# A decoder layer with a mixture of experts: the second half of each expert's weight splitting is moved from VectorE to GpSimd

## The chip, the core and the metric

The kernel runs on one core of a Trainium2 chip, as one program. TensorE (PE in the rows; PEld is its weight load), VectorE (DVE), ScalarE (ACT), GpSimd (POOL) and SyncE (SP) run their own instruction streams and wait for one another by semaphores. The metric is device time in microseconds. Three runs of the kernel before gave 1063.22, 1064.2 and 1065.08 us, a median of 1064.2 us.

## The reference, cut to what matters

One layer: a parallel attention and mLSTM mixer, then a mixture of experts over 1024 tokens of 1024 values, with 16 experts of hidden width 512 and two experts for each token, all in float32. The change lies in the experts:

```python
def hier_moe(x, w_rg, b_rg, w_re, b_re, w_gate, w_up, w_down):
    ...                                  # routing: 2 of 16 experts for each token
    y = jnp.zeros(t.shape, jnp.float32)
    for e in range(N_EXPERTS):
        h = jax.nn.silu(t @ w_gate[e]) * (t @ w_up[e])
        y = y + combine[:, e:e + 1] * (h @ w_down[e]).astype(jnp.float32)
```

## The kernel before, in words

The attention, the mLSTM and the routing take the first 590 us or so and are not touched. Then the experts are worked through in order, 0 to 15. The tokens of an expert are gathered into tiles of 128 rows; an expert has at least one tile. With this input there are 24 tiles: experts 1 to 5, 7, 11 and 12 have two, the other eight (0, 6, 8, 9, 10, 13, 14, 15) have one.

Every product of float32 numbers is made of three matmuls on a high part and a low part (`three`): high by high, high by low, low by high. So each weight is split before it is used. An expert's weights are 12 pieces of 128x1024 values: pieces 0 to 7 are gate and up in turn, pieces 8 to 11 are the four row blocks of the down matrix. For each piece of the next expert:

- SP loads it into a slot (`load_piece`), once the low part of the piece that was there is made (`lo_ready`). SP goes through the pieces in order, so a late piece 11 also holds back the load of the next piece 0.
- ACT copies it, rounded, into `whi` (`w_high` in the rows), once PE has done its last matmul with the piece that `whi` held (`split_hi`, the semaphore `act_hi`).
- DVE subtracts the rounded value from the exact one into `wlo` (`w_low`; `split_lo`, L1628, L1632). Both inputs of this instruction are in SBUF: the slot and `whi`.

All this is done in the last tile of an expert, for the expert that follows; where an expert has two tiles, nothing is split in its first. There are 15 such tiles. The order of a tile on DVE is written out in `tile` (L1635): the product of activation and up for hidden columns 0 to 255 (`hidden`, L1606, `q_sb` in the rows), piece 0, the low part of that half (`hidden_lo`, L1619), piece 1, the other half's product and low part, the low parts of the next tile's rows (`rows_lo`, L1613), pieces 2 to 7, the weighting of the tile's result (`weigh`, L1626), pieces 8 to 11. Pieces 8 to 11 are therefore split while PE is already in the next tile.

PE's tile (L1155) is 24 matmuls of 128x512 for gate and up of hidden columns 0 to 255 (bank J0), 12 of the 24 for the other columns (bank J1), the transposes of the first half of the hidden values (`hidden_T`, L1151, `bank_s`), the other 12, the eight transposes of the next tile's rows (`rows_T`), the transposes of the second half (`bank_x`), and 24 for the down product, six for each of pieces 8 to 11. Before each pair of gate and up pieces and before each down piece it waits for the low part.

POOL's tile (L598) picks the row numbers of the tile after the next, waits until PE has transposed the rows that are in the buffer, issues the gather, waits for the weighted result of ACT and DVE, picks this tile's row numbers and issues the scatter that adds the result into the output. Each wait on a register value is followed by a multiply of one element (`tick`, L525).

Of the kernel before, what the change touches and what calls it, by code (L numbers as in the profile page):

```python
# [5 lines left out]
def hymba_layer_program(nc, x, rel_bias, norm_mix_g, w_in, q_norm_g, k_norm_g, attn_sink, conv_w, conv_b,  # L6
# [15 lines left out]
    F32 = mybir.dt.float32  # L22
# [3 lines left out]
    ALU = mybir.AluOpType  # L26
# [25 lines left out]
    FC = FF // P  # L52
# [11 lines left out]
    with ctx:  # L64
        def sb(name, shape, dt=F32):
            return ctx.enter_context(nc.sbuf_tensor(name, shape, dt))
# [4 lines left out]
        def sems(names):  # L71
            return [ctx.enter_context(nc.semaphore(n)) for n in names.split()]
# [14 lines left out]


        PIECES, PW = 3 * FC, 2 * FF
        OUTP = D // P  # L90
        whi, wlo = sb("w_high", [P, PIECES * PW], F32R), sb("w_low", [P, PIECES * PW], F32R)

        mxh, mxl = sb("rows_high", [P, KC, P], F32R), sb("rows_low", [P, KC, P], F32R)

        MX = [(mxh, mxl), tuple(w[:, OUTP * PW:(OUTP + 1) * PW].rearrange("p (k n) -> p k n", k=KC)
                                for w in (whi, wlo))]
# [6 lines left out]
        def sb1(name, shape):  # L103
# [98 lines left out]
        slot = [*pieces_of(wres, 6), slot_b[:, 0:PW], junk, gffn[:, :], xin[:, 0, :], xin[:, 1, :], h2[:, :]]  # L202
# [39 lines left out]
        (hi0, lo0, act_hnh, dve_hnl) = sems("hi_proj lo_proj act_hn_high dve_hn_low")  # L242

        ld_piece = sems(" ".join(f"ld_piece{j}" for j in range(PIECES)))
        (ld_rows, ld_g, st_y, act_hi, lo_ready_w, pe_mx, pe_gup, pe_hT, pe_dnp, act_silu, act_mx, act_hT, act_y,
         dve_mh, dve_mx, dve_hT, dve_y, pool_rowg, dve_wt) = sems(
            "ld_rows ld_gathered st_y act_hi lo_ready_w pe_mx pe_gateup pe_hT pe_down act_silu act_mx act_hT act_y "
            "dve_mh dve_mx dve_hT dve_y pool_rowg dve_wt")

        block = ctx.enter_context(nc.Block())  # L250
# [1 line left out]
        def wait(eng, sem, value):  # L252

            if not (isinstance(value, int) and value <= 0):
                eng.wait_ge(sem, value)
# [59 lines left out]
        def order(i):  # L315

            return (i % 2) * FC + i // 2 if i < 2 * FC else i

        def lo_ready(e, i):


            return (lo_ready_w, e * PIECES + (i + 1))

        def split_free(i):

# [4 lines left out]
        def _(sp):  # L330
# [68 lines left out]
            def body(t, u, main, nxt, ahead):  # L399
                if main and not nxt:  # L400
# [4 lines left out]
                    sp.wait_ge(dve_hn, TILES)  # L405
                    for i in range(OUTP):
                        if i == OUTP - 1:
                            sp.wait_ge(lo0, PIECES + 1)
# [11 lines left out]
            sp.dma_start(xin[:, 0, :], x2[0:P, :]).then_inc(LDX[0], 16)  # L420
            sp.wait_ge(lo0, PIECES + OUTP)
            sp.dma_start(gffn[:, :], norm_ffn_g[0, :].partition_broadcast(P)).then_inc(ld_gf, 16)
# [61 lines left out]
        def _(pool):  # L484
# [35 lines left out]
            def pwait(sem, value):  # L520

                pool.wait_ge(sem, value)
                if not isinstance(value, int):
                    ticks.append(len(ticks))
                    pool.tensor_tensor(tick[:, len(ticks):len(ticks) + 1], mhalf[0:1, 0:1], mhalf[0:1, 0:1], ALU.mult)  # L525
# [40 lines left out]
            def gather():  # L566
                pool.indirect_dma_start(
                    out=xg[:, :], out_offset=None, in_=ffn_in,
                    in_offset=bass.IndirectOffsetOnAxis(ap=row_g[:, 0:1].bitcast(U32), axis=0)).then_inc(ld_g, 16)

            def scatter_add():
                pool.indirect_dma_start(  # L572
                    out=out, out_offset=bass.IndirectOffsetOnAxis(ap=row_s[:, 0:1].bitcast(U32), axis=0),
                    in_=yb[:, :], in_offset=None, compute_op=ALU.add).then_inc(st_y, 16)

            def pick(dst, t):

                at = tabi[0:1, ROWS + t:ROWS + t + 1] if isinstance(t, int) else tabi[0:1, bass.ds(t + ROWS, 1)]
                col = pool.value_load(at, min_val=0, max_val=TCOLS - 1)
                pool.tensor_copy(dst[:, :], rows[:, bass.ds(col, 1), 0:1].rearrange(  # L580
                    "p a c -> p (a c)")).then_inc(pool_rowg, 1)
# [13 lines left out]
            gather()  # L595
            pool.wait_ge(st_h, 16 * TILES)

            def tile(t):  # L598
                pwait(ld_g, 16 * t + 32)
                pick(row_g, t + 2)  # L600
                pwait(pool_rowg, 2 * t + 3)
                pwait(pe_mx, t + 2)
                gather()
                pwait(act_y, t + 1)
                pwait(dve_y, t + 1)
                pick(row_s, t)
                pwait(pool_rowg, 2 * t + 4)
                scatter_add()

            def inner_tiles(e):  # L610
                first = pool.value_load(tabi[0:1, FIRST + e:FIRST + e + 1] if isinstance(e, int) else
                                        tabi[0:1, bass.ds(e + FIRST, 1)], min_val=0, max_val=MAXT - 1)
                last = pool.value_load(tabi[0:1, LAST + e:LAST + e + 1] if isinstance(e, int) else
                                       tabi[0:1, bass.ds(e + LAST, 1)], min_val=0, max_val=MAXT - 1)
                with pool.If(first < last):
                    with pool.Fori(first, last) as t:
                        tile(t)
                return last

            with pool.Fori(0, NE - 1) as e:  # L620
                tile(inner_tiles(e))
            end = inner_tiles(NE - 1)
            tile(end)
            pwait(st_y, 16 * end + 16)
            pwait(ld_g, 16 * end + 48)

# [2 lines left out]
        def _(act):  # L629
# [16 lines left out]
            def out_high(i):  # L646

                act.wait_ge(ld_piece[i], 32)
                act.wait_ge(pe_om, TILES)
                act.activation(whi[:, i * PW:(i + 1) * PW], slot_out[i], ACT.Copy,  # L650
                               scale=gml[:, i - AW // P:i - AW // P + 1] if i >= AW // P else 1.0).then_inc(hi0, 1)
# [21 lines left out]
            def body(t, u, main, nxt, ahead):  # L673
# [37 lines left out]
                if main:  # L711
# [6 lines left out]
                    if not nxt:  # L718
                        for i in range(4, OUTP):
                            out_high(i)  # L720
# [104 lines left out]
            def split_hi(e, i, last):  # L825

                act.wait_ge(ld_piece[i], e * 16 + (48 if i < OUTP else 32))
                if last is not None:
# [370 lines left out]
        def _(dve):  # L1199
# [402 lines left out]
            def hidden(t, half):  # L1602
                cols = slice(half * HF, (half + 1) * HF)
                dve.wait_ge(act_silu, 2 * t + half + 1)
                wait(dve, pe_hT, 2 * t)
                dve.tensor_tensor(mh[:, cols], sg[:, cols], (J0, J1)[half][:, HF:], ALU.mult).then_inc(dve_mh, 1)  # L1606
# [9 lines left out]
            def hidden_lo(t, half):  # L1616
                dve.wait_ge(act_hT, 2 * t + half + 1)
                at = slice(2 * half, 2 * half + 2)
                dve.tensor_tensor(mhl[:, at, :].rearrange("p a b -> p (a b)"), (S0, X0)[half][:, 0:HF],  # L1619
                                  mhh[:, at, :].bitcast(F32).rearrange("p a b -> p (a b)"), ALU.subtract).then_inc(dve_hT, 1)  # L1620
# [14 lines left out]
            def tile(t, split):  # L1635
                wait(dve, act_y, t)
                wait(dve, dve_y, t)
                col = dve.value_load(tabi[0:1, bass.ds(t + ROWS, 1)], min_val=0, max_val=TCOLS - 1)
                dve.tensor_copy(wt_t[:, 0:1], rows[:, bass.ds(col, 1), 1:2].rearrange("p a c -> p (a c)")
                                .bitcast(F32)).then_inc(dve_wt, 1)  # L1640
                hidden(t, 0)
                split(0, 1)
                hidden_lo(t, 0)
                split(1, 2)
                hidden(t, 1)
                hidden_lo(t, 1)
                rows_lo(t + 1)
                split(2, 2 * FC)
                weigh(t)
                split(2 * FC, PIECES)  # L1650

            def inner_tiles(e):
                first = dve.value_load(tabi[0:1, FIRST + e:FIRST + e + 1] if isinstance(e, int) else
                                       tabi[0:1, bass.ds(e + FIRST, 1)], min_val=0, max_val=MAXT - 1)
                last = dve.value_load(tabi[0:1, LAST + e:LAST + e + 1] if isinstance(e, int) else
                                      tabi[0:1, bass.ds(e + LAST, 1)], min_val=0, max_val=MAXT - 1)
                with dve.If(first < last):
                    with dve.Fori(first, last) as t:
                        tile(t, lambda a, b: None)
                return last  # L1660

            for i in range(2 * FC):
                split_lo(0, i)
            rows_lo(0)
            for i in range(2 * FC, PIECES):
                split_lo(0, i)
            dve.wait_ge(ld_rows, 16)
            with dve.Fori(0, NE - 1) as e:
                last = inner_tiles(e)

                def split(a, b):
                    for i in range(a, b):
                        split_lo(e + 1, i)
# [44 lines left out]
```

## Time and profile before

| | |
|---|---|
| median of three runs | 1064.2 us |
| the profiled execution, its own time | 1064.2 us |
| its span | 1062.4 us |
| PE busy | 948.8 us, 89% |
| DVE busy | 618.2 us, 58% |
| ACT busy | 527.4 us, 50% |
| POOL busy | 246.2 us, 23% |

The span is the time from the first to the last instruction of the core in the profiled execution; the 1.8 us between it and the time are the start and the end of the program. The busy shares are means over the whole program, and the stretch that the change touches is the last 450 us of it. Of the DMA traffic, 169.68 MB in all, the most is weights of the experts: 16 experts of 12 pieces of 512 KB. Spans on POOL are rough.

### The profile page before, as it was taken

The numbers are of one execution on the slowest core, as the hardware profiler recorded it, in microseconds if no ns is written. First come the engines' busy times: TensorE is split into PE (matmuls) and PEld (weight loads), VectorE is DVE, ScalarE is ACT, GpSimd is POOL, SyncE is SP. The second block draws the span as 40 slices with busy tenths as digits, with TensorE's granted clock in tenths as the row PEclk, the third lists the DMA queues.
The fourth block names the chain that finished last, engine by engine and source line by source line (L and its number), as shares of the span: only waits on it lengthen the run. The fifth ranks groups of instructions, "written<-read, shape, count | busy, mean of one in ns | idle before, by whom it ended". The sixth has DMA issues, their size and how long they took to land. (4 is left out here: it accounts for less than half of the span.)

```text
span 1062.4 us, 16918 instructions
## 1 busy us (share of the span) xinstructions
PE 948.8 (89%) x5026; PEld 792.8 (75%) x5027; DVE 618.2 (58%) x1245; ACT 527.4 (50%) x945; POOL 246.2 (23%) x362
## 2 busy tenths in 40 slices
PE   4789999999999969699971799999999999999993
PEld 3678889898888857588861577877877777787772
DVE  3646555656665565343367466447639489754891
ACT  3364644627455373122114356545638488664871
POOL 3101001010110100000017133243234345513452
PEclk9999999999999986899985799999999999999998
DMA  8620010101000050533463788678669799966963
GB/s 259 216 54 20 22 40 0 39 0 39 20 20 20 2 190 9 172 126 134 142 220 102 288 285 255 166 231 289 177 202 339 220 319 395 374 174 202 321 245 60
DMA packets 58122, 169.68 MB, mean 160 GB/s; under 512 B 12744, under 2 KB 15088, under 8 KB 58096
## 3 DMA queue, kind: packets, MB, share of 16 engines
q1 hardware_dynamic: 50384, 143.13, 37.5%
q0 software_dynamic: 7712, 26.24, 10.5%
q8 instruction: 13, 0.21, 0.1%
q14 instruction: 13, 0.11, 0.0%
HBM read 142.96 MB, written 26.38 MB: 159 GB/s over the span
## 5 line engine op out<-in xcount | busy, mean ns | idle before, releaser
L886 PE MATMUL bank_j<-w_high,rows_high 128*128 128x512 f32 x640 | 256.6, 401 | 11.7 <-DVE w_low L1327 9.4
L888 PE MATMUL bank_j<-w_high,rows_low 128*128 128x512 f32 x640 | 251.4, 393 | 0.0
L887 PE MATMUL bank_j<-w_low,rows_high 128*128 128x512 f32 x640 | 251.3, 393 | 0.0
L886 PEld LDWEIGHTS bank_j<-w_high,rows_high 128*128 128x128 f32 x640 | 121.2, 189 | 40.9 <-issue 12.3
L525 POOL TENSOR_TENSOR tick<-mhalf 1x1 f32<-1x1 f32 x146 | 83.9, 577 | 279.1 <-ACT lg L823 136.8
L888 PEld LDWEIGHTS bank_j<-w_high,rows_low 128*128 128x128 f32 x640 | 121.2, 189 | 26.1
L887 PEld LDWEIGHTS bank_j<-w_low,rows_high 128*128 128x128 f32 x640 | 121.6, 190 | 23.7
L1632 DVE TENSOR_TENSOR w_low<-w_res,w_high 128x1024 fp32r<-128x1024 f32 x96 | 112.8, 1219 | 13.8 <-ACT w_high L633 13.8
L633 ACT ACTIVATE w_high<-w_res 128x1024 fp32r<-128x1024 f32 x96 | 96.2, 1059 | 8.4 <-PE bank_j L888 8.0
L880 PE MATMUL bank_t<-ident,hn 128*128 128x128 f32 x328 | 45.1, 283 | 33.8 <-DMA hn<-ffn_in,row_g 22.2
L880 PEld LDWEIGHTS bank_t<-ident,hn 128*128 128x128 f32 x328 | 40.0, 146 | 39.0 <-issue 34.8
L982 PE MATMUL bank_j<-hnT,w_res 128*128 128x128 f32 x512 | 63.7, 285 | 1.5 <-DMA w_res<-in_w_in_dram 1.5
L982 PEld LDWEIGHTS bank_j<-hnT,w_res 128*128 128x128 f32 x512 | 61.9, 201 | 2.8 <-DMA w_res<-in_w_in_dram 1.9
L1606 DVE TENSOR_TENSOR q_sb<-cy,bank_j 128x256 f32<-128x256 f32 x48 | 20.1, 419 | 71.1 <-ACT cy L803 71.1
L530 POOL TENSOR_TENSOR rqk<-ssqk,eps_hd 128x10 f32<-128x10 f32 x8 | 5.8, 728 | 224.8 <-DVE ssqk L1423 224.8
L803 ACT ACTIVATE cy<-bank_j 128x256 f32<-128x256 f32 x48 | 18.1, 377 | 72.1 <-PE bank_j L888 72.1
L572 POOL DMA_INDIRECT out_dram<-lg,row_s x24 | 50.6, 2108 | 5.9 <-issue 5.9
L669 ACT ACTIVATE lg<-lg,anm 128x256 f32<-128x256 f32 x64 | 31.7, 497 | 34.1 <-DVE aes L1352 34.1
L633 ACT ACTIVATE w_high<-bias 128x1024 fp32r<-128x1024 f32 x36 | 36.3, 1065 | 7.5 <-DMA bias<-in_w_in_dram 7.5
L886 PE MATMUL bank_s<-w_high,hidden_high 128*128 128x512 f32 x96 | 39.9, 416 | 0.0
L633 ACT ACTIVATE rows_high<-bank_t 128x512 fp32r<-128x512 f32 x58 | 31.4, 599 | 15.2 <-PE bank_t L880 15.2
L1632 DVE TENSOR_TENSOR w_low<-bias,w_high 128x1024 fp32r<-128x1024 f32 x32 | 37.7, 1222 | 0.0
(301 smaller groups left out, 1823.0 us busy)
## 6 DMA issues: line engine op xcount, KB each, us to landing
w_res<-in_w_gate_dram SPq DMA_DIRECT2D x48, 512.0 KB, 4.9
w_res<-in_w_up_dram SPq DMA_DIRECT2D x48, 512.0 KB, 5.4
bias<-in_w_down_dram SPq DMA_DIRECT2D x32, 512.0 KB, 5.6
slot_b<-in_w_gate_dram SPq DMA_DIRECT2D x16, 512.0 KB, 5.7
PT<-in_w_up_dram SPq DMA_DIRECT2D x16, 512.0 KB, 5.9
gmix<-in_w_down_dram SPq DMA_DIRECT2D x16, 512.0 KB, 5.5
h<-in_w_down_dram SPq DMA_DIRECT2D x16, 512.0 KB, 7.2
hn<-in_x_dram SPq DMA_DIRECT2D x8, 512.0 KB, 3.5
```

Of the source, the lines that this page charges most:

```text
L525: pool.tensor_tensor(tick[:, len(ticks):len(ticks) + 1], mhalf[0:1, 0:1], mhalf[0:1, 0:1], ALU.mult)
L572: pool.indirect_dma_start(out=out, out_offset=bass.IndirectOffsetOnAxis(ap=row_s[:, 0:1].bitcast(U32), axis=0), in_=yb[:, :], in_offset=No ...
L633: return act.activation(dst, src, ACT.Copy)
L669: act.activation(pr[:, j, :], lg[:, j, :], ACT.Exp, bias=anm[:, h:h + 1], accum_out=asum[:, h:h + 1])
L803: act.activation(sg[:, half * HF:(half + 1) * HF], (J0, J1)[half][:, 0:HF], ACT.Silu).then_inc(act_silu, 1)
L880: ins = pe.transpose(TB[b][:, i * P:(i + 1) * P], src[:, (4 * b + i) * P:(4 * b + i + 1) * P], ident[:, :])
L886: pe.matmul(out_, ah, bh, start=start, stop=False)
L887: pe.matmul(out_, ah, bl, start=False, stop=False)
L888: return pe.matmul(out_, al, bh, start=False, stop=stop)
L982: ins = pe.matmul(J0[:, c * P:(c + 1) * P], wi[:, k, KVG + c * P:KVG + (c + 1) * P], hnT[:, k, :], start=(k == 0), stop=(k == KC - 1))
L1606: dve.tensor_tensor(mh[:, cols], sg[:, cols], (J0, J1)[half][:, HF:], ALU.mult).then_inc(dve_mh, 1)
L1632: dve.tensor_tensor(wlo[:, at], slot[i], whi[:, at].bitcast(F32), ALU.subtract).then_inc(lo_ready(e, i)[0], 1)
```

## The change

The low parts of pieces 8 to 11 of experts 1 to 15 are made by POOL, and no longer by DVE. POOL makes them behind the scatter of the tile in which DVE made them. Those of expert 0 stay on DVE. The low parts have two semaphores, `lo_a` for pieces 0 to 7 and `lo_b` for pieces 8 to 11, each with a count of its own, since two engines now signal them. The instruction is the same: 128x1024 values, one input in the slot and one in `whi`.

```diff
+        VP = 2 * FC
...
         def lo_ready(e, i):
-            return (lo_ready_w, e * PIECES + (i + 1))
+            return (lo_a, e * VP + (i + 1)) if i < VP else (lo_b, e * (PIECES - VP) + (i - VP + 1))
...
-            def tile(t):
+            def tile(t, split):
                 pwait(ld_g, 16 * t + 32)
                 pick(row_g, t + 2)
                 pwait(pool_rowg, 2 * t + 3)
                 pwait(pe_mx, t + 2)
                 gather()
+                split(VP, 2 * FC)
                 pwait(act_y, t + 1)
                 pwait(dve_y, t + 1)
                 pick(row_s, t)
                 pwait(pool_rowg, 2 * t + 4)
                 scatter_add()
+                split(2 * FC, PIECES)
...
             with pool.Fori(0, NE - 1) as e:
-                tile(inner_tiles(e))
+                last = inner_tiles(e)
+
+                def split(a, b):
+
+                    for i in range(a, b):
+                        pool.wait_ge(act_hi, e * PIECES + (PIECES + i + 1))
+                        at = slice(order(i) * PW, order(i) * PW + PW)
+                        pool.tensor_tensor(wlo[:, at], slot[i], whi[:, at].bitcast(F32),
+                                           ALU.subtract).then_inc(lo_ready(e + 1, i)[0], 1)
+                tile(last, split)
...
-                split(2, 2 * FC)
+                split(2, VP)
                 weigh(t)
-                split(2 * FC, PIECES)
```

`VP` is 8, as `2 * FC` is, so the first `split` on POOL is empty and the second makes pieces 8 to 11. The last lines are those of `tile` on DVE.

POOL's stream at the end of an expert's last tile, before: the tile's result is waited for, its row numbers are picked (`row_s`), the scatter is issued, and the loop over the experts turns (L620, L611).

```order
L525 TENSOR_TENSOR tick<-mhalf 1x1 [waits dve_y]
L579 ISA
L579 TENSOR_LOAD tabi
L579 ISA x2
L580 ISA
L580 COPY row_s<-rows 128x1
L522 REGISTER_ALU
L525 TENSOR_TENSOR tick<-mhalf 1x1 [waits pool_rowg]
L572 DMA out_dram<-lg,row_s 1152x1024
L620 REGISTER_ALU
```

The same place in the changed kernel, from the last tick before the scatter:

```order
L526 TENSOR_TENSOR tick<-mhalf 1x1 [waits pool_rowg]
L573 DMA out_dram<-lg,row_s 1152x1024
L629 ISA
L631 TENSOR_TENSOR w_low<-gmix,w_high 128x1024 [waits act_hi]
L629 REGISTER_ALU
L631 TENSOR_TENSOR w_low<-bias,w_high 128x1024 [waits act_hi]
L629 REGISTER_ALU
L631 TENSOR_TENSOR w_low<-bias,w_high 128x1024 [waits act_hi]
L629 REGISTER_ALU
L631 TENSOR_TENSOR w_low<-h,w_high 128x1024 [waits act_hi]
L623 REGISTER_ALU
```

Four subtractions of 128x1024 stand between the scatter and the turn of the loop, and so ahead of the next tile's gather.

DVE's stream at the same end of a tile, before, from the weighting of the result (`lg`) on:

```order
L1626 TENSOR_SCALAR lg<-bank_o,wt_t 128x512 [waits st_y]
L1630 REGISTER_ALU
L1632 TENSOR_TENSOR w_low<-gmix,w_high 128x1024 [waits act_hi]
L1630 REGISTER_ALU
L1632 TENSOR_TENSOR w_low<-bias,w_high 128x1024 [waits act_hi]
L1630 REGISTER_ALU
L1632 TENSOR_TENSOR w_low<-bias,w_high 128x1024 [waits act_hi]
L1630 REGISTER_ALU
L1632 TENSOR_TENSOR w_low<-h,w_high 128x1024 [waits act_hi]
L1668 REGISTER_ALU
```

And in the changed kernel:

```order
L1644 TENSOR_TENSOR w_low<-PT,w_high 128x1024 [waits act_hi]
L1635 REGISTER_ALU
L1637 REGISTER_ALU [waits dve_wt,pe_down]
L1638 TENSOR_SCALAR lg<-bank_o,wt_t 128x512 [waits st_y]
L1679 REGISTER_ALU
```

The four subtractions behind the weighting are gone; the loop turns right after it, and the next instructions with work are the copy of the weights and the first `hidden` product of the next tile.

## Rows read from the trace of the kernel before

**Rows 1.** busy by stretch: length, PE PEld DVE ACT POOL, clock, DMA, GB/s

```profile
604.00:1050.00 446.00, 426.55 (x1983) 345.89 (x1981) 293.01 (x370) 276.33 (x392) 167.32 (x237) 1.00 0.79 259
857.10:876.40 19.30, 18.20 (x86) 14.67 (x85) 17.20 (x21) 15.99 (x22) 9.55 (x10) 1.00 1.00 352
912.90:950.20 37.30, 36.17 (x170) 29.45 (x169) 21.22 (x30) 20.55 (x31) 12.45 (x20) 1.00 0.76 246
```

**Rows 2.** waits: line, what it waited for: us, times, longest

```profile
PE bank_s L1151 <- DVE q_sb L1606: 15.5, 15, 1.1
```

**Rows 3.** the chain that ended last: start, us, what

```profile
866.50 0.44 PE bank_s L1151 x2
```

**Rows 4.** timeline of PE: start, us, engine, line, what [idle before]

```profile
857.13 0.39 PE L886 MATMUL bank_j<-w_high,rows_high 128*128 128x512 f32 x1
866.50 0.44 PE L1151 MATMUL bank_s<-ident,q_sb 128*128 128x128 f32 x2 [1.05 <-DVE q_sb L1606]
870.61 0.44 PE L1151 MATMUL bank_x<-ident,q_sb 128*128 128x128 f32 x2
870.81 0.49 PE L886 MATMUL bank_s<-w_high,hidden_high 128*128 128x512 f32 x1
876.39 0.39 PE L886 MATMUL bank_j<-w_high,rows_high 128*128 128x512 f32 x1
```

**Rows 5.** timeline of DVE, the same tile

```profile
860.76 0.75 DVE L1626 TENSOR_SCALAR lg<-bank_o,wt_t 128x512 f32<-128x512 f32 x1
861.42 1.22 DVE L1632 TENSOR_TENSOR w_low<-gmix,w_high 128x1024 fp32r<-128x1024 f32 x1
864.83 1.22 DVE L1632 TENSOR_TENSOR w_low<-h,w_high 128x1024 fp32r<-128x1024 f32 x1
866.35 1.22 DVE L1632 TENSOR_TENSOR w_low<-w_res,w_high 128x1024 fp32r<-128x1024 f32 x1
870.13 0.42 DVE L1606 TENSOR_TENSOR q_sb<-cy,bank_j 128x256 f32<-128x256 f32 x1 [1.09 <-ACT cy L803]
871.99 1.29 DVE L1613 TENSOR_TENSOR rows_low<-bank_t,rows_high 128x512 fp32r<-128x512 f32 x2
873.20 4.62 DVE L1632 TENSOR_TENSOR w_low<-w_res,w_high 128x1024 fp32r<-128x1024 f32 x4
```

**Rows 6.** timeline of ACT, the same tile

```profile
863.72 0.36 ACT L803 ACTIVATE cy<-bank_j 128x256 f32<-128x256 f32 x1
864.13 2.01 ACT L633 ACTIVATE w_high<-w_res 128x1024 fp32r<-128x1024 f32 x2
```

**Rows 7.** timeline of POOL while DVE splits

```profile
861.59 1.10 POOL L525 TENSOR_TENSOR tick<-mhalf 1x1 f32<-1x1 f32 x1 [1.83 <-DVE lg L1626]
862.64 1.18 POOL L580 COPY row_s<-rows 128x1 int32 x1
```

**Rows 8.** timeline of DVE, then POOL, where the expert has a second tile

```profile
708.33 0.75 DVE L1626 TENSOR_SCALAR lg<-bank_o,wt_t 128x512 f32<-128x512 f32 x1 [3.40 <-PE bank_o L888]
710.73 1.60 POOL L572 DMA_INDIRECT out_dram<-lg,row_s  x1 [0.39 <-issue]
```

**Rows 9.** POOL by form: count, busy us, mean ns, idle before

```profile
L530 POOL TENSOR_TENSOR hrs<-hss,eps_dv 128x4 f32<-128x4 f32 x8 | 1.6, 203 | 122.5 <-DVE hss L1475 122.5
L530 POOL TENSOR_TENSOR rsh<-ssh,eps_d 128x1 f32<-128x1 f32 x8 | 1.5, 189 | 116.8 <-ACT PT L791 116.8
L497 POOL TENSOR_SCALAR_AFFINE_SELECT selh<-selh 4x512 f32<-4x512 f32 x1 | 0.6, 634 | 0.1
L501 POOL TENSOR_SCALAR_AFFINE_SELECT selp<-selp 4x256 f32<-4x256 f32 x1 | 0.4, 407 | 0.1
```

**Rows 10.** DMA issues: KB each where known, median us to landing

```profile
h<-in_w_down_dram SPq DMA_DIRECT2D x16, 512.0 KB, 7.2
hn<-ffn_in,row_g POOLq DMA_INDIRECT x26, 5.3
```

**Rows 11.** the scatter on POOL: count, min/median/max ns, first and last start

```profile
L572 POOL DMA_INDIRECT out_dram<-lg,row_s x24: 1584/2407/2435, 622.2 to 1049.9; - x24
```

More of the change, by code:

```diff
@@ L244, in hymba_layer_program @@
         ld_piece = sems(" ".join(f"ld_piece{j}" for j in range(PIECES)))
-        (ld_rows, ld_g, st_y, act_hi, lo_ready_w, pe_mx, pe_gup, pe_hT, pe_dnp, act_silu, act_mx, act_hT, act_y,
+        (ld_rows, ld_g, st_y, act_hi, lo_a, lo_b, pe_mx, pe_gup, pe_hT, pe_dnp, act_silu, act_mx, act_hT, act_y,
          dve_mh, dve_mx, dve_hT, dve_y, pool_rowg, dve_wt) = sems(
-            "ld_rows ld_gathered st_y act_hi lo_ready_w pe_mx pe_gateup pe_hT pe_down act_silu act_mx act_hT act_y "
+            "ld_rows ld_gathered st_y act_hi lo_a lo_b pe_mx pe_gateup pe_hT pe_down act_silu act_mx act_hT act_y "
             "dve_mh dve_mx dve_hT dve_y pool_rowg dve_wt")
@@ L616, in inner_tiles @@
                     with pool.Fori(first, last) as t:
-                        tile(t)
+                        tile(t, lambda a, b: None)
                 return last
             with pool.Fori(0, NE - 1) as e:
-                tile(inner_tiles(e))
+                last = inner_tiles(e)
[6 more added lines that the diff above has]
+                tile(last, split)
             end = inner_tiles(NE - 1)
-            tile(end)
+            tile(end, lambda a, b: None)
             pwait(st_y, 16 * end + 16)
@@ L1660, in inner_tiles @@
                 return last
-            for i in range(2 * FC):
+            for i in range(VP):
                 split_lo(0, i)
             rows_lo(0)
-            for i in range(2 * FC, PIECES):
+            for i in range(VP, PIECES):
                 split_lo(0, i)
```

## The prediction

> **What bounds the kernel now.** I read the busy time by stretch first. In the 446 us of the experts PE is busy for 426.55 us at a granted clock of 1.00, the higher of its two levels (2.4 GHz), DVE for 293.01 and POOL for 167.32 [rows 1]. PE sets the time, then, and only what PE waits for counts. The list of waits names one such wait in this stage: the transposes of the first half of the hidden values wait for DVE's product, 15 times, 15.5 us in all [rows 2]. Fifteen is the number of tiles that come right behind a tile in which weights were split. The chain that ended last goes through the same transposes [rows 3].
>
> The timelines of one tile show why. PE starts it at 857.13 and stands still for 1.05 us before 866.50 [rows 4]. DVE had the result weighted at 860.76 to 861.51, then split pieces 8 to 11, the last from 864.83 to about 865.96, and only then could make the product, though ACT's half of it was there at 863.72 + 0.36 = 864.08 [rows 5, 6]. PE wanted the product by 866.50 - 1.05 = 865.45. The tile takes 876.39 - 857.13 = 19.26 us, 1.05 of which is the gap, so 18.2 without it [rows 4].
>
> **What the change removes.** Four subtractions of about 1.14 us (861.42 to the next DVE work at 864.83 is three of them, 3.41 us) leave DVE ahead of the product [rows 5]. The product can then be made as soon as ACT is ready, 864.1 to 864.5, which is 0.9 us ahead of PE. ACT's own work is unchanged and comes no later. The whole gap of 1.05 us closes, in 15 tiles: -15.8 us. Behind it the next limit is PE itself.
>
> **What it adds: when POOL can start.** POOL splits behind the scatter. Where DVE does not split, the scatter is issued at 710.73 and ends at 712.33, which is 3.25 us after DVE ended the weighting (708.33 + 0.75 = 709.08) [rows 8]. In the changed kernel DVE is idle there too, so in the tile above POOL starts piece 8 at 861.51 + 3.25 = 864.76.
>
> **How long one piece takes on POOL.** The trace has no such instruction. From below: one with a single input costs 634 ns for 512 elements and 407 for 256, 0.887 ns an element, so 0.18 + 0.91 = 1.09 us for 1024. From above: the addition of two inputs costs 203 ns for 4 elements and 189 for 1, 4.7 ns an element, so 5.0 us for 1024 [rows 9]. The first slope is taken over 256 elements and the second over three, so I stay near the first: with two inputs read one behind the other it gives 0.18 + 2 x 0.91 = 2.0 us. With 0.3 us for starts, ends and the handing over from piece to piece, I take 2.3 us as the spacing, an estimate. The Trainium skill (GPSIMD Engine Reference, Elementwise side by side) has 4497 ns for a two-input addition of 2048 elements, so an estimate of 2.25 us for 1024; the sum below would be about 1 us lower by it. No row here shows it.
>
> **What lies behind POOL's pieces.** PE needs piece 8 + c at the c-th step of the down product. That product is 24 matmuls in 876.39 - 870.81 = 5.58 us, 0.2325 each [rows 4]. Without the gap it starts at 869.76 and asks for piece 11 after 18 matmuls, at 873.95. POOL has piece 11 at 864.76 + 4 x 2.3 = 873.96. So at 2.3 us a piece it just fits; each 0.1 us more costs 0.4 us in each tile, and at 2.56 us the gain of 1.05 is used up. POOL's gather comes 5 us later than now, lands in 5.3 us [rows 10], and is read a tile of 18 us later: hidden. SP's load of piece 11 waits for POOL and lands 7.2 us later [rows 10]. If POOL ends at 876.2 (below), it lands at 883.4, about 1.5 us late for ACT in a one-tile expert, inside PE's new slack of 0.9 and a little more. I count it at nothing, and at up to 0.5 us in the six tiles in the range.
>
> **What both engines want at once.** POOL's small instructions show a shared resource. An addition of one element takes 189 ns by itself [rows 9]; the tick, a multiply of one element, starts at 861.59 and ends at 862.69; DVE's split of piece 8 ends at 861.42 + 1.22 = 862.64. The copy behind it, from 862.64, takes 1.18 us, one DVE split again [rows 5, 7]. So a POOL instruction that reads SBUF waits until a DVE subtraction with both inputs in SBUF has ended, and gets its turn before the next. The trace cannot show the reverse, since POOL has no long reads. Its bounds are: DVE is never held (nothing), or DVE's split is held for a whole POOL piece (2.3 us). One resource that holds POOL back for whole instructions will most simply do the same to DVE; I take the second.
>
> The Trainium skill (SBUF, State Buffer; Who interferes with whom) says that a DVE instruction with two SBUF inputs contends with a GpSimd instruction that reads SBUF, and that whoever issues first holds the pair for its whole instruction. For POOL's side the trace agrees (1.10 us against 0.19); for DVE's side no row exists. By this rule the sum is the one below, without it the faster rival.
>
> Where does DVE split beside POOL? Only where the tile behind an expert's last is itself a last tile: experts 6, 8, 9, 10, 13 and 14, six tiles. Nine tiles have no DVE split beside POOL's: the first tiles of experts 1 to 5, 7, 11 and 12, and expert 15. (Of the 24 scatters [rows 11], nine take about 1.6 us, as the one in rows 8: the eight first tiles of two, and the last tile.)
>
> **The walk through such a tile**, with the times above:
> - POOL piece 8: 864.76 to 867.06. DVE's piece 0 has its high part at 864.13 + 1.05 = 865.2 [rows 6], is held until 867.06 and ends at 868.20 (now: from 866.35).
> - POOL piece 9 to 870.50. DVE's piece 1 is held until then and ends at 871.64. The second product stands behind it on DVE: 871.64 instead of 870.13 [rows 5]. PE had no slack there (bank_x at 870.61 right behind the product). The first gap was closed, so PE arrives 1.05 early and waits 2.56: the tile is 1.5 us longer than now.
> - POOL piece 10 to 873.94, piece 11 to 876.24; PE asks for it at 876.51. DVE's piece 2 is ready at 874.8 and held until 876.24 instead of 873.20 [rows 5]. Six pieces later, at 883.05, piece 7 is there; the next tile started at 877.90 and wants it at 882.09: 0.96 us of wait.
>
> In the tile behind, POOL starts at 883.80 + 3.25 = 887.05. If nothing is split there by DVE (experts 7, 11, 15), POOL ends at 896.25 and PE asks at 873.95 - 857.13 = 16.82 after its start, plus 0.96, at 895.68: 0.57 of wait. The tile takes 18.2 + 0.96 + 0.57 = 19.7, 0.5 more than now. If DVE splits there too (experts 9, 10, 14), its piece 0 comes first (885.95 to 887.09), then POOL 8 to 889.39, DVE 1 to 890.53, POOL 9 to 892.83, POOL 10 to 895.13, DVE 2 to 896.27, POOL 11 to 898.57. PE asks for piece 10 at 894.28 and for piece 11 at 896.52, waits 0.85 and 2.05, and ends at 898.57 + 1.40 = 899.97. The tile takes 22.07, 2.8 more than now; for the third in a row I take the same.
>
> **Sum.** Experts 6, 8, 13: 3 x 1.5 = 4.5. Experts 9, 10, 14: 3 x 2.8 = 8.4. Experts 7, 11, 15: 3 x 0.5 = 1.5. Experts 1 to 5 and 12: 6 x -1.05 = -6.3. Together +8.1 us. The profiled execution took 1064.2 us (a span of 1062.4), the same as the median of the runs: 1064.2 + 8.1 = 1072.3, so 1072 us.
>
> **Rivals.** A change of 0.2%, about 2.1 us, is what a measurement of this kernel can tell from none.
> - Faster: DVE is not held by POOL. Then every tile is as in the nine, and at up to 2.3 us a piece the gain is whole: 1064.2 - 15.8 = 1048.4 us. At 2.45 us it is 15 x (1.05 - 0.6), 1057. A short POOL piece comes to the same with holding: at 1.1 us DVE's piece 1 is out by about 868.5, before 869.1, when the second product would be wanted, and the time is 1049. For it: only POOL's side of the holding is in the rows. Against it: POOL's side is plain there.
> - Slower by POOL's own speed, with no holding needed: the place is PE's wait for piece 11, the price four times the excess over 2.3, and it decides from 2.56 us on. At 2.75 us it is 15 x (1.8 - 1.05) = +11, with holding about +30 (1094); at the upper bound of 5.0 us it is 15 x (10.8 - 1.05) = +146. For it: the 4.7 ns an element of the small additions. Against: that slope rests on three elements.
> - Cancelled: near 2.1 us a piece with holding, each held tile is about 0.4 to 0.8 us shorter, and the 8.1 us shrink to nothing.
> - The holding is not taken in turns: POOL runs its four pieces together, and DVE's piece 0 waits until 873.96. The second product is then about 6 us late in six tiles: about +30.
>
> **Chances.** Forecast (holding, turns, 2.15 to 2.5 us) 0.47; faster rival 0.32; cancelled 0.08; slower by POOL's speed or without turns 0.13. The forecast's own range is 1067 to 1084. The range for all, 1048 to 1090, takes in the faster rival's 1048.4 and leaves out the far part of the last case. Faster by over 0.2%: 0.32; within: 0.08; slower: 0.60.
>
> **What would show it.** The wait of the first transposes for the product (15.5 us) gone. A POOL subtraction of 128x1024 with a mean near 2.3 us, four in a row in the nine tiles. In the six tiles DVE's pieces 0, 1 and 2 longer than 1.22 us or late by a POOL piece, and PE waiting at the second transposes and for low parts in the down product. Two-tile experts should take 36.4 us for two tiles instead of 37.3 [rows 1], one-tile experts 20.8 to 22.1 instead of 19.3. I am wrong if DVE's splits keep 1.22 us and their place beside POOL's, or if POOL's piece is over 2.6 us, when the two-tile experts too get longer.

## The result, and the profile after

The changed kernel takes 1100.86 us (median of 4 runs, 1100.78 to 1103.79), the kernel before 1064.64 beside it (4 runs, 1063.22 to 1066.13): a ratio of 1.0361, interval 1.0339 to 1.0382. It is slower, 29 us beyond the 1072 us forecast, and outside the range of 1048 to 1090. The medians differ by 36.2 us. The profiled execution has a span of 1103.3 us, 40.9 more than the one before, so it is some 5 us longer against its own median than that one; the readings below are of this execution.

Busy time in the stage of the experts (columns as in rows 1). The stage and what ends it now take 487 us where [rows 1] had 446:

```profile
604.00:1091.00 487.00, 439.66 (x1999) 357.67 (x1997) 276.39 (x311) 277.54 (x393) 258.88 (x298) 0.96 0.78 239
```

PE stands still for 487 - 439.66 = 47.3 us, before for 19.45, and is busy 13.1 us longer. Some 3.6 of these are work of expert 0, which comes 3.6 us later here and so has 16 more matmuls in the window. For the rest the work is the same, but the granted clock has a mean of 0.96 where it had 1.00. So there are two losses, one of waits and one of clock. The list of waits (line, what it waited for: us, times, longest) names the first:

```profile
PE bank_x L1163 <- DVE q_sb L1618: 42.1, 6, 7.7
```

The wait for the first product of [rows 2], 15 times, is gone. In its place six waits for the second product have come, up to 7.7 us each. They are in six tiles: those of experts 6, 8, 9, 10, 13 and 14.

What stands ahead of that product on DVE. POOL's timeline of expert 9's tile, then DVE's (columns as in rows 4):

```profile
896.47 1.61 POOL L573 DMA_INDIRECT out_dram<-lg,row_s  x1 [0.37 <-issue]
897.54 2.98 POOL L631 TENSOR_TENSOR w_low<-gmix,w_high 128x1024 fp32r<-128x1024 f32 x1
899.90 5.30 POOL L631 TENSOR_TENSOR w_low<-bias,w_high 128x1024 fp32r<-128x1024 f32 x2
904.65 2.84 POOL L631 TENSOR_TENSOR w_low<-h,w_high 128x1024 fp32r<-128x1024 f32 x1
907.08 1.53 POOL L581 COPY row_g<-rows 128x1 int32 x1
```

```profile
899.12 0.42 DVE L1618 TENSOR_TENSOR q_sb<-cy,bank_j 128x256 f32<-128x256 f32 x1 [3.15 <-ACT cy L815]
900.64 7.94 DVE L1644 TENSOR_TENSOR w_low<-w_res,w_high 128x1024 fp32r<-128x1024 f32 x1 [1.10 <-ACT w_high L645]
908.84 1.21 DVE L1644 TENSOR_TENSOR w_low<-w_res,w_high 128x1024 fp32r<-128x1024 f32 x1
909.97 0.41 DVE L1618 TENSOR_TENSOR q_sb<-cy,bank_j 128x256 f32<-128x256 f32 x1
```

POOL's four pieces form one run from 897.54 to 904.65 + 2.84 = 907.49. They start (907.49 - 2.84 - 897.54) / 3 = 2.37 us apart, but one lasts 2.98, so each starts before the one ahead of it has ended. DVE's piece 0, a subtraction of 1.22 us in [rows 5], lasts 7.94: it ends at 908.58, 1.09 behind POOL's run, about its own length. So this subtraction, with both inputs in SBUF, got nothing done beside the whole run. DVE's product at 899.12, which has one input in a bank of PSUM, lay beside the same run and took its usual 0.42. In the tile ahead (expert 8) the same subtraction lasts 9.96, and in that of expert 6 it lasts 9.97, the longest of 96:

```profile
L1644 DVE TENSOR_TENSOR w_low<-w_res,w_high x96: 1204/1218/9972, 578.7 to 1069.0; 128x1024 fp32r<-128x1024 f32 x96
```

(Count, then min/median/max in ns.) The second loss stands right behind such a wait. PE's timeline in the tile of expert 8, and the windows there (length, PE, PEld, DVE, ACT, POOL, granted clock, DMA share, GB/s):

```profile
884.43 0.69 PE L1163 MATMUL bank_x<-ident,q_sb 128*128 128x128 f32 x2 [7.72 <-DVE q_sb L1618]
885.78 0.63 PE L900 MATMUL bank_s<-w_high,hidden_low 128*128 128x512 f32 x1
886.20 0.63 PE L898 MATMUL bank_o<-w_high,hidden_high 128*128 128x512 f32 x1
889.82 0.39 PE L898 MATMUL bank_s<-w_high,hidden_high 128*128 128x512 f32 x1
```

```profile
866.00:876.00 10.00, 10.00 (x48) 8.21 (x47) 6.83 (x6) 8.78 (x12) 7.18 (x7) 1.00 0.98 307
876.70:884.40 7.70, 0.02 (x1) 0.00 (x0) 7.68 (x4) 0.00 (x0) 7.46 (x8) 0.67 0.68 243
884.40:889.30 4.90, 4.87 (x13) 3.91 (x14) 3.66 (x5) 4.14 (x7) 0.88 (x1) 0.50 0.90 308
```

The granted clock falls while PE stands still and is 0.50 (1.2 GHz) when it starts again. The down product's matmuls then start 0.43 us apart instead of 0.2275; here eleven do so, in the tile of expert 9 six. From the start of the second transposes to the next tile's first matmul it is 7.1 to 8.1 us in the six tiles and 5.77 where the clock stays at 1.00: 1.4 to 2.3 us more in each, 10.7 together.

Where DVE splits nothing beside POOL, nothing of this shows. The second tile of expert 1, on POOL and then on PE:

```profile
624.91 2.99 POOL L631 TENSOR_TENSOR w_low<-gmix,w_high 128x1024 fp32r<-128x1024 f32 x1
632.02 2.90 POOL L631 TENSOR_TENSOR w_low<-h,w_high 128x1024 fp32r<-128x1024 f32 x1
```

```profile
634.98 0.50 PE L898 MATMUL bank_s<-w_high,hidden_high 128*128 128x512 f32 x1 [0.34 <-POOL w_low L631]
```

Measured from one tile's first matmul to the next's, the tiles behind a split took 19.25 us before. Now the six of experts 1 to 5 and 12 take 18.6 (-3.8 together), those of experts 7, 11 and 15 take 18.0 (-3.6), and the six held ones 27.4, 28.0, 25.0, 26.7, 27.1 and 26.5 (+45.1). The sum is +37.6. Another 3.6 us is there before POOL splits anything (the second tile starts at 617.8 instead of 614.2), and the rest, -0.3, lies in the other tiles and behind the last one. The 3.6 are no price of POOL's subtractions: the traces of e1_signal, e3_write and e5_copy have this start at 616.4, 614.3 and 614.6, with no other code ahead of it. What moves it no run shows.

### The profile page after: what moved, and what is told of

The parts are those of the page before. It is cut to its first block, busy times and chain, and to the rows that moved or that the text cites. A ratio compares the mean times of both kernels' runs of the same rounds, so it can differ in the third digit from the quotient of the medians.

```text
span 1103.3 us, 16918 instructions
## 1 busy us (share of the span) xinstructions
PE 962.4 (87%) x5026; PEld 805.0 (73%) x5027; DVE 601.2 (54%) x1185; ACT 527.5 (48%) x945; POOL 337.8 (31%) x422
## 4 chain that ended last, share of the span: by engine, by line
PE 24%; issue 9%; POOL 7%; ACT 5%; DVE 2%; POOLq 2%; DMA 1%; ACTq 0%; DVEq 0%
PE bank_j L898 5%; PE bank_j L900 5%; PE bank_j L899 5%; POOL w_low L631 4%; ACT w_high L645 3%; POOL table L539 2%; PE bank_s L898 1%; DVE w_low L1644 1%; PE bank_s L899 1%; PE bank_s L900 1%; PE bank_o L898 1%; PE bank_o L899 1%; PE bank_o L900 1%; POOL tick L526 1%; PE bank_x L1163 1%
## 5 line engine op out<-in xcount | busy, mean ns | idle before, releaser
L1644 DVE TENSOR_TENSOR w_low<-w_res,w_high 128x1024 fp32r<-128x1024 f32 x96 | 161.1, 1720 | 19.2 <-ACT w_high L645 19.2
L898 PEld LDWEIGHTS bank_j<-w_high,rows_high 128*128 128x128 f32 x640 | 121.8, 190 | 39.6 <-issue 12.4
L526 POOL TENSOR_TENSOR tick<-mhalf 1x1 f32<-1x1 f32 x146 | 51.1, 357 | 206.3 <-ACT lg L835 106.8
L631 POOL TENSOR_TENSOR w_low<-bias,w_high 128x1024 fp32r<-128x1024 f32 x30 | 79.3, 2932 | 0.0
L892 PE MATMUL bank_t<-ident,hn 128*128 128x128 f32 x328 | 45.1, 283 | 35.8 <-DMA hn<-ffn_in,row_g 24.3
L815 ACT ACTIVATE cy<-bank_j 128x256 f32<-128x256 f32 x48 | 18.1, 377 | 72.1 <-PE bank_j L900 72.1
L1163 PE MATMUL bank_x<-ident,q_sb 128*128 128x128 f32 x48 | 12.0, 337 | 43.2 <-DVE q_sb L1618 42.1
L898 PE MATMUL bank_s<-w_high,hidden_high 128*128 128x512 f32 x96 | 43.3, 451 | 1.9 <-POOL w_low L631 1.9
L631 POOL TENSOR_TENSOR w_low<-gmix,w_high 128x1024 fp32r<-128x1024 f32 x15 | 44.8, 2984 | 0.0
L631 POOL TENSOR_TENSOR w_low<-h,w_high 128x1024 fp32r<-128x1024 f32 x15 | 43.2, 2882 | 0.0
```

What stands on the lines that cost most here:

```text
L631: pool.tensor_tensor(wlo[:, at], slot[i], whi[:, at].bitcast(F32), ALU.subtract).then_inc(lo_ready(e + 1, i)[0], 1)
L892: ins = pe.transpose(TB[b][:, i * P:(i + 1) * P], src[:, (4 * b + i) * P:(4 * b + i + 1) * P], ident[:, :])
L898: pe.matmul(out_, ah, bh, start=start, stop=False)
L1163: ins = pe.transpose((S0, X0)[half][:, c * P:(c + 1) * P], mh[:, half * HF + c * P:half * HF + (c + 1) * P], ident[:, :])
L1644: dve.tensor_tensor(wlo[:, at], slot[i], whi[:, at].bitcast(F32), ALU.subtract).then_inc(lo_ready(e, i)[0], 1)
```

## The experiments

All but two were timed beside the kernel before. Its median was 1065.18 us (8 runs) for the first four below, and 1066.5 (11 runs) for the others. A time stands as median, range and ratio with its interval.

**e1_signal: the gap alone.** POOL subtracts one element of each piece and signals. The rest of the low parts is left out.

```
-  pool.tensor_tensor(wlo[:, at], slot[i], whi[:, at].bitcast(F32),
+  pool.tensor_tensor(wlo[0:1, order(i) * PW:order(i) * PW + 1], slot[i][0:1, 0:1],
```

> Left out: POOL makes only the first element of the low parts of pieces 8 to 11 of experts 1 to 15; the rest of them is not made. Everything else of the changed kernel stays: order, waits, signals. This is the change without the price of POOL's work. Step of the prediction: the gap of 1.05 us in 15 tiles closes and nothing comes in its place, 1048.4 us (ratio to before 0.985). If instead the slowdown comes from the new order of signals, loads or the gather on POOL, it stays above 1064.

Measured: 1047.33 us (1044.46 to 1047.75), ratio 0.9821 (0.9797 to 0.9845). No tile from the second on is over 18.04, none has a wait, and DVE's split has its old length:

```profile
876.72 1.22 DVE L1644 TENSOR_TENSOR w_low<-w_res,w_high 128x1024 fp32r<-128x1024 f32 x1 [0.70 <-ACT w_high L645]
```

The order of the work, the signals, the late gather and the late loads cost nothing. All of the loss inside the tiles comes from POOL's length and what it holds. The gap was worth 1.2 us a tile and not the 1.05 that the wait shows: the wait is counted from the modelled end of the last matmul (0.39 us), while matmuls in a row start 0.23 apart.

**e2_serial: POOL's run broken up.** POOL waits for its own last piece before each next one.

```
+  pool.wait_ge(lo_b, (e + 1) * (PIECES - VP) + (i - VP))
```

> POOL waits for the end of each of its pieces before it starts the next, so its four no longer overlap. Theory A (the port passes from POOL piece to POOL piece because the next has begun to read before the last has ended, and any gap lets DVE in): DVE's piece 0 takes at most about 3 us plus its own 1.2 instead of 8 to 10; the two-tile experts get longer, since four pieces one by one take about 3.1 us each (12.4 instead of 10 us): about 2.9 us more wait for piece 11 in nine tiles. The one-tile experts take about 23.5 us instead of 26.5. Sum about 1064 + 40, near 1105. Theory B (DVE is out as long as POOL has a piece in its queue): DVE's piece 0 stays at 10 us and more, one-tile experts over 28 us, sum over 1125.

Measured: 1081.26 us (1079.35 to 1081.61), ratio 1.0141 (1.012 to 1.0163). POOL, then DVE, in one tile:

```profile
867.71 2.97 POOL L632 TENSOR_TENSOR w_low<-gmix,w_high 128x1024 fp32r<-128x1024 f32 x1
870.76 6.63 POOL L632 TENSOR_TENSOR w_low<-bias,w_high 128x1024 fp32r<-128x1024 f32 x2
```

```profile
868.76 3.02 DVE L1645 TENSOR_TENSOR w_low<-w_res,w_high 128x1024 fp32r<-128x1024 f32 x1 [0.71 <-ACT w_high L646]
872.04 3.07 DVE L1645 TENSOR_TENSOR w_low<-w_res,w_high 128x1024 fp32r<-128x1024 f32 x1
```

POOL's second piece now starts behind the end of the first (870.68), and here the turns are taken as forecast: DVE's piece 0 comes in between, and is out at 871.78 instead of behind the run. PE waits 2.6 to 2.9 us for the second product. Behind this wait the clock stays at 1.00 in two of the six tiles and is at 0.50 for about 3 us in four. In those two PE waits 1.0 us for a low part at the start of the next tile instead. One wait that adds time to POOL makes the kernel 20 us faster than the changed one, and shows that it is the unbroken run that keeps DVE out.

The turns came out as expected, the time did not: 1105 was expected. The nine tiles were to lose 2.9 us each against the changed kernel, but they take 19.0 to 19.6, which is 0.4 us more in six and 1.1 to 1.4 in three. The expectation took 3.1 us for every piece. Only the first lasts 2.97 to 3.0; the later ones last 2.4 and start 2.5 apart where DVE is not in between (3.3 where it is), so that a run in the nine tiles is 10.45 us long and not 12.4. The six tiles take 21.9 to 22.5 instead of about 23.5.

**e4_late: DVE's splits moved away.** Pieces 0 and 1 stand behind the low parts of the rows.

```
-  split(0, 1)
-  split(1, 2)
-  split(2, VP)
+  split(0, VP)
```

> DVE makes its pieces 0 and 1 behind the second product and the next tile's rows, in front of piece 2. If the six long tiles are long because the second product stands behind the held piece 0 on DVE, PE's wait for that product (5.7 to 7.7 us, six times) goes, and comes back smaller as a wait for low parts of gate and up: pieces 0 to 7 then end about 27 us after the tile's start, and PE wants the last at 22.4. One-tile experts about 20.6 to 22.5 us instead of 25 to 28, but the nine others lose 2 to 4 us where their low parts of gate and up come late. Sum 1085 to 1100. If PE is held by POOL's pieces themselves (wait for low parts in the down product), nothing gets shorter: 1101 or more.

Measured: 1098.98 us (1097.31 to 1099.48), ratio 1.0309 (1.0287 to 1.0331). No wait for a product is left, so the six tiles shrink to 22.0 to 22.4. But the gate product of the next tile now waits for low parts, in the nine tiles too, which grow to 20.9 to 21.4:

```profile
PE bank_j L898 <- DVE w_low L1644: 25.5, 42, 1.0
```

The loss has a place only because pieces 0 and 1 stand ahead of the product; taken from there they are late for their own reader. The down product waits for POOL's low parts as well, 15 times, 7.2 us in all. The two kinds of wait together are 32.7 us, the 15 tiles are 52 longer than in e1_signal; the rest was not traced to a row.

**e6_one: one piece on POOL.** DVE splits 8, 9 and 10 behind the weighting.

```
-  VP = 2 * FC
+  VP = 3 * FC - 1
...
-  split(2, VP)
+  split(2, 2 * FC)
   (the weighting)
+  split(2 * FC, VP)
```

> Only piece 11 is made by POOL, behind the scatter; DVE keeps 8 to 10 behind the weighting. Theory (the price is the length of POOL's run of pieces against the place of DVE's piece 0 and 1): the run is one piece of 3 us instead of four in 10 us. DVE's first product is ready in time or 0.1 us late, so up to 1.05 us are gained in each of 15 tiles; in six tiles a DVE piece is held by up to 3 us, the second product is up to 1.2 us later than before. Sum 1064.6 - 9.5 - 0 to +7: 1050 to 1060. If every POOL reading in this place costs a fixed price by itself, it is over 1065.

The same constant orders what DVE makes for expert 0, ahead of the stage: pieces 8 to 10 of expert 0 now come in front of the low parts of its rows, where 0 to 7 stood.

Measured: 1058.62 us (1057.44 to 1061.64, 5 runs), ratio 0.994 (0.992 to 0.996): 0.6% faster than before. The nine tiles take 18.1 us, the six 19.3. POOL, DVE and PE in one of the six:

```profile
883.92 2.98 POOL L630 TENSOR_TENSOR w_low<-h,w_high 128x1024 fp32r<-128x1024 f32 x1
```

```profile
884.54 3.45 DVE L1643 TENSOR_TENSOR w_low<-w_res,w_high 128x1024 fp32r<-128x1024 f32 x1
```

```profile
888.38 0.44 PE L1162 MATMUL bank_x<-ident,q_sb 128*128 128x128 f32 x2 [1.21 <-DVE q_sb L1617]
```

DVE's piece 1 ends at 887.99, 1.09 behind POOL's 886.90, and the product stands behind it.

The three pieces of expert 0 cost time of their own. POOL's copy of the first tile's row numbers stands beside them, and the first gather behind it:

```profile
580.79 9.37 POOL L588 COPY row_g<-rows 128x1 int32<-128x1 int32 x1 [3.25 <-DMA rows<-table]
```

```profile
587.76 2.34 DVE L1643 TENSOR_TENSOR w_low<-bias,w_high 128x1024 fp32r<-128x1024 f32 x2
```

This copy lasts 5.79 us in the changed kernel, and ends 0.05 us behind DVE's last split in both. PE's wait for the first gather goes from 24.3 us to 27.6. Three more splits at 1.14 us from start to start are 3.4 us of this time, an estimate, that belong to expert 0 and not to the number of pieces on POOL. In e7_one_later it is the same (a wait of 28.3 us), in e8_two it is two splits, 2.3 us (27.4). The 15 tiles alone are 10.4 us shorter than before.

**e8_two: two pieces on POOL.** As e6_one, with VP = 3 * FC - 2.

> Pieces 10 and 11 on POOL, 8 and 9 on DVE: a run of two. If the length of the hold is the length of what is left of POOL's run (2.4 us a piece, the last 3), DVE's held piece takes up to 5.3 + 1.2 us (10 in the changed kernel, 3.4 with one piece), and the six tiles about 21 to 22 us instead of 25 to 28; the nine others 18.1. Sum 1064.6 - 10 + 6 x 2.5 = about 1068 (1062 to 1074). If a hold ends at the latest after one POOL piece, as many pieces as there may be, 1058 as with one piece.

Measured: 1081.2 us (1079.56 to 1081.98), ratio 1.0136 (1.0107 to 1.0164), slower than expected. POOL, DVE, PE and the windows ahead of and behind PE's wait:

```profile
868.38 2.99 POOL L630 TENSOR_TENSOR w_low<-bias,w_high 128x1024 fp32r<-128x1024 f32 x1
870.77 2.90 POOL L630 TENSOR_TENSOR w_low<-h,w_high 128x1024 fp32r<-128x1024 f32 x1
```

```profile
868.30 6.46 DVE L1643 TENSOR_TENSOR w_low<-w_res,w_high 128x1024 fp32r<-128x1024 f32 x1 [0.69 <-issue]
```

```profile
876.62 0.69 PE L1162 MATMUL bank_x<-ident,q_sb 128*128 128x128 f32 x2 [4.21 <-DVE q_sb L1617]
```

```profile
872.30:876.60 4.30, 0.10 (x1) 0.00 (x0) 4.26 (x4) 0.00 (x0) 4.06 (x6) 0.91 1.01 276
876.60:882.30 5.70, 5.68 (x15) 4.54 (x16) 4.48 (x6) 4.96 (x7) 0.86 (x1) 0.50 0.98 336
```

Two overlapping pieces already act as one hold: DVE's piece 0 ends at 874.76, again 1.09 behind POOL's run (873.67). It loses though its row starts 0.08 us ahead of POOL's. In e6_one piece 0 was all but done when POOL's only piece began (out at 884.20, 0.28 us behind that start); here it waits for the whole of two, and PE's wait goes from 1.2 to 4.2 us in four of the six tiles (2.7 and 1.7 in the others). What the expectation of 1068 lacked is mostly the clock, at 0.50 in the 5.7 us behind the wait: it costs 1.6 to 2.8 us in each of the four tiles, 9.5 together. The steps are 1, 2 and 4 pieces: 1058.6, 1081.2, 1100.9 us.

**e3_write: POOL writes and does not read** (one run). Its low parts are set to zero, the subtraction is left out; the wait before each piece is now the one with a small multiply behind it.

```
-  pool.tensor_tensor(wlo[:, at], slot[i], whi[:, at].bitcast(F32),
-                     ALU.subtract).then_inc(lo_ready(e + 1, i)[0], 1)
+  pool.memset(wlo[:, at].bitcast(F32), 0.0).then_inc(lo_ready(e + 1, i)[0], 1)
```

> Left out: the low parts of pieces 8 to 11 of experts 1 to 15 are set to zero by POOL (a write of 128x1024 with no input) instead of being computed. Four writes of about 1 us each, each behind a one-element tick that waits. If what both engines share is the read side, DVE's pieces 0 and 1 in the six tiles stay at 1.22 us. If it is any access of POOL, the piece 0 that meets the run is longer by up to 1 to 4 us. Time about 1048 either way.

Measured: 1045.57 us in one run. POOL, then DVE:

```profile
891.86 1.45 POOL L631 MEMSET w_low<- 128x1024 f32 x1
892.78 1.27 POOL L526 TENSOR_TENSOR tick<-mhalf 1x1 f32<-1x1 f32 x1
893.99 0.94 POOL L631 MEMSET w_low<- 128x1024 f32 x1
```

```profile
892.77 1.23 DVE L1643 TENSOR_TENSOR w_low<-w_res,w_high 128x1024 fp32r<-128x1024 f32 x1 [0.70 <-ACT w_high L644]
```

DVE's split keeps 1.23 us beside POOL's writes of the same tiles, and no wait appears. The tick, which reads, waits for DVE's split to end as in [rows 7].

**e5_copy: one long read instead of two** (one run). POOL copies the slot and subtracts nothing, with the same wait as e3_write.

```
-  pool.tensor_tensor(wlo[:, at], slot[i], whi[:, at].bitcast(F32),
-                     ALU.subtract).then_inc(lo_ready(e + 1, i)[0], 1)
+  pool.tensor_copy(wlo[:, at], slot[i]).then_inc(lo_ready(e + 1, i)[0], 1)
```

> Left out: POOL copies the exact weights of pieces 8 to 11 of experts 1 to 15 into their low parts (one input of 128x1024 in SBUF) instead of subtracting. Four copies of about 1.1 us with a tick before each. If one long read on POOL is enough to hold DVE, DVE's piece 0 or 1 in the six tiles takes 2 us or more; if only a POOL instruction with two inputs does so, they stay at 1.22 us. Time 1048 to 1052.

Measured: 1064.14 us in one run. POOL, then DVE:

```profile
880.72 1.51 POOL L631 CAST w_low<-gmix 128x1024 fp32r<-128x1024 f32 x1
881.73 0.50 POOL L526 TENSOR_TENSOR tick<-mhalf 1x1 f32<-1x1 f32 x1
881.86 1.41 POOL L631 CAST w_low<-bias 128x1024 fp32r<-128x1024 f32 x1
884.13 1.21 POOL L631 CAST w_low<-h 128x1024 fp32r<-128x1024 f32 x1
```

```profile
883.21 3.21 DVE L1643 TENSOR_TENSOR w_low<-w_res,w_high 128x1024 fp32r<-128x1024 f32 x1 [1.11 <-ACT w_high L644]
```

A piece takes 1.14 us from start to start, half of the subtraction's 2.37, and the run is 4.6 us long. DVE's piece, begun in its middle, ends at 886.42, 1.08 behind the run's end at 885.34. So one long input read by POOL holds DVE as well, and the length of the run sets the price. In the tile shown (expert 9) PE waits 1.0 us. In the five others DVE's piece 0 lasts 4.8 us and PE waits 2.5 to 2.6. Of these, the three with a clock of 0.50 behind the wait take 22.1 us, the two without 20.5.

**e7_one_later: the version that the others point to.** As e6_one, and DVE's piece 1 stands behind the second product, ahead of that product's low part (`hidden_low`).

```
-  split(1, 2)
   hidden(t, 1)
+  split(1, 2)
```

> As with piece 11 alone on POOL, and DVE makes its piece 1 behind the second product instead of in front of it. With piece 11 alone, six tiles still waited 1.2 us for the second product, behind a piece 1 that POOL held for one of its own pieces. If that is all that is left of the price, all 15 gaps are closed: 19.25 us tiles become 18.1, 15 x 1.15 = 17 us less than before: about 1048, the time of the kernel in which POOL only signals (1047.3). If the wait moves to the low part of the second half of the hidden values or to the next tile's rows, 1052 to 1058.

Measured: 1051.41 us (1049.7 to 1054.23, 6 runs), ratio 0.9857 (0.9834 to 0.9879). POOL, then DVE:

```profile
883.74 2.97 POOL L630 TENSOR_TENSOR w_low<-h,w_high 128x1024 fp32r<-128x1024 f32 x1
```

```profile
882.78 1.23 DVE L1643 TENSOR_TENSOR w_low<-w_res,w_high 128x1024 fp32r<-128x1024 f32 x1
886.89 1.22 DVE L1643 TENSOR_TENSOR w_low<-w_res,w_high 128x1024 fp32r<-128x1024 f32 x1
```

POOL's piece now lies between two splits of DVE but for 0.27 us, in which neither is longer than alone, and all tiles from the second on take 18.0 to 18.15. No wait for a product or a low part of the weights is left, so the whole price of the tiles is gone. That the time is not the expected 1048 is expert 0's 3.4 us (e6_one): 1051.4 - 3.4 = 1048.0, an estimate; no run has the one piece on POOL and the old order for expert 0. It is faster than both kernels, by 1.4% and about 4.5% (1051.41 / 1100.86; these two did not run side by side).

## Why the prediction was wrong

**The gap closes: right.** All 15 waits are gone, and e1_signal gives 17.9 us for it where 15.8 stood.

**When POOL starts: nearly right.** Piece 8 starts at 624.91, 2.75 us behind the weighting's end (621.42 + 0.74), where 3.25 was forecast.

**How long a piece takes: right in spacing, wrong in its end.** The spacing is 2.37 us (forecast 2.3). But a piece lasts 2.9 to 3.0, so the last ends 0.6 later than its spacing says, and that end is what PE waits for. In six of the nine tiles this leaves a wait of 0.30 to 0.34, and the tile gains 0.64 instead of 1.05. The other three, experts 7, 11 and 15, gain 1.2 where the walk had them lose 0.5: they stand behind a tile that is 7 us or more longer than before, and nothing is late in them. The small edits counted at nothing were nothing.

**Which tiles are held, and where it hurts: right.** They are the six tiles named, and the place is the second product.

**What both engines want at once: the failed step.** The prediction said that a held engine "gets its turn before the next" instruction of the other, and took that for DVE too. Its evidence, [rows 7], shows only POOL waiting, and POOL's two small instructions wait once for each DVE split. For DVE the profile after shows the opposite: while POOL's instructions overlap, DVE has no turn until the run has ended. e2_serial breaks the run and gets the turns; e8_two and e5_copy show that two pieces, or copies, suffice for the hold; e3_write shows that it is not POOL's writing.

The trace of before already had a row against the turns, which the prediction did not read. POOL's copy of the first row numbers, which has one column and takes 0.18 us elsewhere, starts while DVE makes eight splits of expert 0 in a row (575.91 to 585.07):

```profile
579.30 5.82 POOL L587 COPY row_g<-rows 128x1 int32<-128x1 int32 x1 [3.39 <-DMA rows<-table]
```

```profile
583.86 1.21 DVE L1632 TENSOR_TENSOR w_low<-PT,w_high 128x1024 fp32r<-128x1024 f32 x1
```

It ends at 585.12, 0.05 behind the last of them and not behind the first: a whole run held it. In all ten traces it ends there. So a hold over a run was seen before the change, with DVE as the one that holds, and "gets its turn before the next" was true of [rows 7] and not of this row.

This was the last rival, "not taken in turns", priced at about +30 and given a small part of 0.13. The six waits add up to 42.1 us, so its mechanism was the right one, and its price of about 6 us a tile near the 5.7 to 7.7 measured.

**What no case had: PE's clock.** After 5.7 to 7.7 us of standing still the down product starts at 0.50, and costs 1.4 to 2.3 us more in each of the six tiles. The sum for these tiles is 42.1 of waits, 10.7 for the clock, less 6 x 1.24 for the gap and less 0.3, since a tile without a wait has 0.05 of idle time at this place too: 45.1. Less 7.5 for the nine tiles it gives the 37.6.

The Trainium skill (SBUF, State Buffer; Who interferes with whom) has DVE with two SBUF inputs contend with a GpSimd instruction that reads SBUF and not with one that only writes. The runs agree with both halves (e5_copy, e3_write). It speaks of one instruction and a second that waits for its end. By that alone DVE's piece would have lasted at most 2.98 + 1.09 = 4.1 us; the rows show 7.94 and 9.96, and the measurement decides.

## What to carry to other kernels

Before giving work to POOL, list what DVE reads with two SBUF inputs while POOL's whole run lasts, and what stands behind that on DVE: the price here was the rest of the run, not one instruction. Keep POOL's reads few and put them between DVE's two-input work, or leave a break between them, which e2_serial shows to be worth 20 us here. A contention seen in one direction says nothing on the other: bound the unseen one by the whole run, and add what PE's clock loses behind a wait of that length. Look for holds in the whole trace, the start of the program too: the row that spoke against the turns stood there, and a constant moved for the tiles cost 3.4 us there.

## What was not expected of the hardware

- POOL's overlapping reads keep DVE out for their whole run: 7.94 us for an instruction of 1.22, ending 1.09 behind the run (1.08 or 1.09 behind a POOL instruction or run in each of the 48 held subtractions of after, e2_serial, e4_late, e5_copy, e6_one and e8_two).
- Who gets a turn is not settled by the runs. DVE's splits follow each other without a break, and POOL's small reads in the tiles wait for one of them each ([rows 7]), but the copy at 579.30 in before waits for all that are left of the eight. And POOL's small `row_g` copy starts at 907.08 by its row, before the run's end at 907.49, yet it ends only at 908.61, with DVE's split. What makes the difference no run shows.
- PE's granted clock behind a wait for the second product, over all runs: 0.50 behind each of the ten of 4.2 to 7.7 us; 1.00 behind each of the eight of 1.0 to 1.7 us; behind the twelve of 2.5 to 2.9 us it fell to 0.50 in seven and stayed at 1.00 in five. Waits of the same 2.55 us went both ways, so their length alone does not decide it.
- A POOL subtraction of 128x1024 lasts 2.8 to 3.0 us and is followed by the next after 2.37. When each waits for the last (e2_serial), the first is followed after 3.07, and the later ones last 2.4 and start 2.5 apart, 3.3 with a DVE split in between.
